# Three-product fp32r features for the last three heads of the mixer, split by ScalarE and GpSimd into the weight ring

## The reference, cut to what matters

```python
mod = cond @ w_ada[l] + b_ada[l]            # 6 x 1024 columns; the second block has 2 x 6144 more
h = modulate(x, norm1_w[l], shift1, scale1)
proj = h @ w_in                             # 256 x 1024 by 1024 x 3592
aq, ak, av, dqkv, dz, db, da = jnp.split(proj, IN_SPLITS, axis=-1)
attn_out = dilated_attention(aq, ak, av)    # 8 heads of 64
dqkv = silu(causal_short_conv(dqkv, conv_w))
o = gated_delta_rule(dq, dk, dv, g, beta)   # 4 heads of 128, chunks of 64
o = rms_norm(o, dn_norm_w) * silu(dz)
x = x + gate1 * (concat([attn_out, dn_out]) @ w_out)
```

## Time and profile before

| | us |
|---|---|
| median of 3 runs | 2387.39 (2383.18 to 2388.57) |
| profiled execution | 2388.36 |
| its span | 2386.6 |
| TensorE busy, whole span | 2180.7 |
| VectorE, ScalarE, GpSimd busy | 1373.6, 642.1, 123.7 |
| bytes moved | 711.73 MB, mean 298 GB/s |

### The profile page before, as it was taken

How to read it: one execution, slowest core, us unless ns; L and a number is a source line. 1 busy time by engine, 2 the same in 40 slices (tenths; PEclk the granted TensorE clock), 3 DMA queues, 4 the chain that set the end, 5 groups by cost and what they waited for, 6 DMA issues and landing times.

```text
span 2386.6 us, 40025 instructions
## 1 busy us (share of the span) xinstructions
PE 2180.7 (91%) x16396; PEld 1515.0 (63%) x16396; DVE 1373.6 (58%) x2654; ACT 642.1 (27%) x814; POOL 123.7 (5%) x203
## 2 busy tenths in 40 slices
PE   7998989998898998988999889899989999998998
PEld 5887842454545444445544555677769888876987
DVE  2455554634453443565545456866678676678866
ACT  1121120121222221311111111444443334445332
POOL 0000010000000000000000000000000000011000
PEclk9999989999999999999999999999989999999999
DMA  9778779998999999999999999444446533334651
GB/s 381 296 292 338 308 290 375 414 420 361 419 419 419 417 419 419 416 418 419 407 419 419 404 413 392 164 154 139 154 142 210 188 129 118 105 115 159 212 183 64
DMA packets 111244, 711.73 MB, mean 298 GB/s; under 512 B 12481, under 2 KB 13137, under 8 KB 36129
## 3 DMA queue, kind: packets, MB, share of 16 engines
q1 hardware_dynamic: 85904, 616.93, 65.4%
q0 software_dynamic: 25168, 92.38, 10.3%
HBM read 705.06 MB, written 4.19 MB: 297 GB/s over the span
## 4 chain that ended last, share of the span: by engine, by line
PE 67%; DVE 15%; DMA 13%; ACT 3%; issue 2%; SPq 0%; DVEq 0%; ACTq 0%
PE bank L313 17%; PE bank L2286 7%; PE bank L2267 6%; PE bank L1999 4%; PE bank L2037 4%; DMA hT<-in_panels_e 3%; PE bank L1662 3%; DMA cst<-in_panels_e 3%; PE bank L1512 2%; DMA ring<-in_units_a 2%; PE bank L2372 2%; DMA hid<-in_panels_e 2%; PE bank L2152 2%; PE bank L2014 2%; PE bank L2141 1%
## 5 line engine op out<-in xcount | busy, mean ns | idle before, releaser
L313 PE MATMUL bank<-hT,scratch 128*32 128x512 f32 x976 | 303.4, 609 | 11.9 <-DMA hT<-in_panels_e 10.0
L313 PE MATMUL bank<-hid,scratch 128*32 128x512 f32 x1008 | 308.0, 606 | 6.2 <-DMA hT<-in_panels_e 3.7
L1265 ACT CAST chi<-craw 128x1024 fp32r<-128x1024 f32 x128 | 133.6, 1045 | 550.9 <-DMA craw<-in_panels_m 214.2
L3290 DVE TENSOR_TENSOR clo<-craw,chi 128x1024 fp32r<-128x1024 f32 x128 | 156.0, 1222 | 158.8 <-ACT chi L1265 157.8
L313 PE MATMUL bank<-yacc,scratch 128*32 128x512 f32 x648 | 179.1, 609 | 5.0 <-DMA diag_gtmp<-in_panels_e 5.0
L313 PE MATMUL bank<-rows,scratch 128*32 128x512 f32 x632 | 172.9, 606 | 9.4 <-DMA cst<-in_panels_e 9.4
L313 PE MATMUL bank<-diag_gtmp,scratch 128*32 128x512 f32 x648 | 177.2, 600 | 2.2 <-DMA hid<-in_panels_e 1.5
L313 PE MATMUL bank<-cst,scratch 128*32 128x512 f32 x632 | 176.6, 608 | 2.4 <-DMA yacc<-in_panels_e 2.4
L1999 PE MATMUL bank<-cT_hi,chi 128*128 128x256 f32 x384 | 112.2, 292 | 17.4 <-DVE crot_lo L3264 6.1
L313 PEld LDWEIGHTS bank<-hT,scratch 128*32 128x32 f32 x976 | 70.7, 112 | 64.4 <-issue 63.8
L1999 PE MATMUL bank<-cT_lo,chi 128*128 128x256 f32 x384 | 109.2, 284 | 0.0
(11 more groups left out here) (680 smaller groups left out, 5680.3 us busy)
## 6 DMA issues: line engine op xcount, KB each, us to landing
hid<-in_panels_e SPq DMA_DIRECT2D x96, 1024.0 KB, 13.4
hT<-in_panels_e SPq DMA_DIRECT2D x94, 1024.0 KB, 13.5
ring<-in_units_a SPq DMA_DIRECT2D x88, 1024.0 KB, 7.1
ring<-in_panels_m SPq DMA_DIRECT2D x64, 1024.0 KB, 5.1
yacc<-in_panels_e SPq DMA_DIRECT2D x48, 1024.0 KB, 11.8
diag_gtmp<-in_panels_e SPq DMA_DIRECT2D x48, 1024.0 KB, 14.3
rows<-in_panels_e SPq DMA_DIRECT2D x47, 1024.0 KB, 13.2
cst<-in_panels_e SPq DMA_DIRECT2D x47, 1024.0 KB, 13.0
```

The costliest lines, as they stand in the source:

```text
L313: m = self.pe.matmul(b[s:s + STRIP, :], lhs(k)[:, s:s + STRIP], v, start=(first and k == 0), stop=(k == KT - 1))
L1265: act.copy(chi[:, h % 2, :], context_raw(h)).then_inc(cx_hi, 1)
L3290: tt(context_lower(h), context_raw(h), chi[:, h % 2, :], ALU.subtract).then_inc(cx_lo, 1)
```

## The change

For heads 1 to 3 the four halves of `first` and `second`, and for all four heads the feature half of `last_columns`, are computed with three fp32r products in place of one fp32 product: 16 halves, listed in `FEATURE_HALVES` in the order in which TensorE uses them. Head 0's first and second, all `tokens` products and all ada products stay in fp32. The tokens are split once: ScalarE copies `hT` into `x_hi`, GpSimd subtracts into `x_lo`, in two parts each. Each half of a weight is split when its unit has landed: ScalarE copies it into one of three places `first_hi`, GpSimd subtracts raw minus upper into `ring_lo[n % 4]`, and TensorE waits for GpSimd (`lower_in`) in place of the landing. ScalarE waits before the copy for the landing and for the use of the half three before it. The copies stand at fixed places of ScalarE's order: last of head 0 and first of head 1 ahead of the loop over j; second of head j + 1 between the Silus and Sqrt of j; last of j + 1 and first of j + 2 behind the Exp of the scores of j. `last_columns` does its tokens before its features. The later counts of `lower_in` and `upper_ready` are moved up by 18, and GpSimd's clearing of `b1raw` waits for the last changed unit, as `first_hi` lies in the same place.

```diff
@@ -73,6 +73,17 @@
+def feature_unit(kind, i):
+    return 8 + 12 * i + {"first": 0, "second": 6, "last": 9}[kind]
...
+FEATURE_HALVES = [(feature_unit(kind, i), half) for i in range(DN_HEADS)
+                  for kind, halves in (("first", 2), ("second", 2), ("last", 1)) if i or kind == "last" for half in range(halves)]
+ROW_PARTS = 2
+FRONT_PARTS = ROW_PARTS + len(FEATURE_HALVES)
...
 def first_units():
@@ -444,6 +455,8 @@
         ring_lo = sb("ring_lo", 4, UNIT, dt=F32R)
+        with ExitStack() as raw:
+            first_hi = raw.enter_context(nc.sbuf_tensor("first_hi", [P, 3, KT, P], F32R))
         with ExitStack() as raw:
@@ -462,6 +475,8 @@
         gateb = sb("gateb", 2, D)
+        with ExitStack() as stages:
+            x_lo = stages.enter_context(nc.sbuf_tensor("x_lo", [P, KT, SEQ], F32R))
         lnrow = sb("lnrow", 2, D)
@@ -569,6 +584,15 @@
         units = ring.rearrange("p s k (h n) -> p (s k h n)", h=2).rearrange("p (u k n) -> p u k n", u=4, k=KT)
+        x_hi = hT_lo[:, :, SEQ:512]
+        def first_parts(n, half):
+            lower = ring_lo[:, n % 4, :].rearrange("p (k n) -> p k n", k=KT)[:, :, P * half:P * half + P]
+            return first_hi[:, FEATURE_HALVES.index((n, half)) % 3], lower
+        def first_raw(n, half):
+            return units[:, n % 4, :, P * half:P * half + P]
@@ -1036,18 +1060,28 @@
+            for h in range(ROW_PARTS):
+                s = slice(4 * h, 4 * h + 4)
+                pool.wait_ge(upper_ready, h + 1)
+                pool.tensor_tensor(x_lo[:, s, :], hT[:, s, 0:SEQ], x_hi[:, s, :], ALU.subtract).then_inc(lower_in, 1)
+            for q, (n, half) in enumerate(FEATURE_HALVES):
+                upper, lower = first_parts(n, half)
+                pool.wait_ge(upper_ready, ROW_PARTS + q + 1)
+                pool.tensor_tensor(lower, first_raw(n, half), upper, ALU.subtract).then_inc(lower_in, 1)
             pool.wait_ge(b2_go, 1)
...
+            pool.wait_ge(unit_used, FEATURE_HALVES[-1][0] + 1)
             pool.memset(b1raw[64:P, :], 0.0).then_inc(filled, 1)
...
             for t in range(XT):
-                pool.wait_ge(upper_ready, t + 1)
+                pool.wait_ge(upper_ready, FRONT_PARTS + t + 1)
                 pool.tensor_tensor(xr_lo[:, t, :], xn[:, t, :], xr_hi[:, t, :], ALU.subtract).then_inc(lower_in, 1)
-            pool.wait_ge(lower_in, XT)
+            pool.wait_ge(lower_in, FRONT_PARTS + XT)
             pool.wait_ge(b1_upper, 1)
@@ -1161,6 +1195,21 @@
+            def upper_features(number):
+                for q in number:
+                    n, half = FEATURE_HALVES[q]
+                    act.wait_ge(first_in[n % 4], 16 * (n // 4 + 1))
+                    if q >= 3:
+                        act.wait_ge(unit_used, FEATURE_HALVES[q - 3][0] + 1)
+                    act.copy(first_parts(n, half)[0], first_raw(n, half)).then_inc(upper_ready, 1)
+            def halves_of(kind, i):
+                return [q for q, (n, _) in enumerate(FEATURE_HALVES) if n == feature_unit(kind, i)]
+            act.wait_ge(odd_feat.free, 2 + KT // 2)
+            act.wait_ge(side.free, 3 + KT // 2)
+            for h in range(ROW_PARTS):
+                act.copy(x_hi[:, 4 * h:4 * h + 4, :], hT[:, 4 * h:4 * h + 4, 0:SEQ]).then_inc(upper_ready, 1)
             act.wait_ge(small_in, 96)
@@ -1171,11 +1220,15 @@
             to_dve.send(act.activation(gates[:, 6, :], gates[:, 6, :], ACT.Exp))
+            upper_features(halves_of("last", 0) + halves_of("first", 1))
             for j in range(DN_HEADS):
+                more = j + 1 < DN_HEADS
                 asked.get()
                 to_tensor.send(act.activation(cs[:, :, :], cy[:, :, :], ACT.Silu))
+                if more:
+                    upper_features(halves_of("second", j + 1))
                 asked.get()
@@ -1187,6 +1240,10 @@
                 to_tensor.send(m)
+                if more:
+                    upper_features(halves_of("last", j + 1))
+                if j + 2 < DN_HEADS:
+                    upper_features(halves_of("first", j + 2))
@@ -1670,11 +1727,25 @@
+            def split_features(b, dst, n, half):
+                pe.wait_ge(lower_in, ROW_PARTS + FEATURE_HALVES.index((n, half)) + 1)
+                upper, lower = first_parts(n, half)
+                for k in range(KT):
+                    for c, (w, x) in enumerate(((upper, x_hi), (upper, x_lo), (lower, x_hi))):
+                        m = pe.matmul(b[:, dst:dst + SEQ], w[:, k, :], x[:, k, :], start=(k == c == 0), stop=(k == KT - 1 and c == 2))
+                return m
             def feature_pair(ready=lambda k: None):
...
                 G.close(features(b, SEQ, v, P), True)
+            def split_pair():
+                b = G.open()
+                n = G.panels.n
+                split_features(b, 0, n, 0)
+                G.close(split_features(b, SEQ, n, 1), True)
@@ -1685,9 +1756,9 @@
                 b = G.open()
-                v = first_unit(KT)
-                features(b, 0, v, 0)
-                G.close(tokens(b, SEQ, v, P), True)
+                n = G.panels.n
+                tokens(b, SEQ, first_unit(KT), P)
+                G.close(split_features(b, 0, n, 0), True)
@@ -1752,8 +1823,10 @@
                 later = 4 * i + 4
-                if more:
-                    feature_pair(*([] if i else [first_feature]))
+                if more and i:
+                    split_pair()
+                elif more:
+                    feature_pair(first_feature)
                 if i >= 2:
@@ -2089,7 +2164,7 @@
             from_experts.get()
-            pe.wait_ge(lower_in, XT)
+            pe.wait_ge(lower_in, FRONT_PARTS + XT)
             gather()
             turn_gathered(0)
```

## The result

| | changed | kernel before, runs beside it |
|---|---|---|
| median, us | 2397.57 (2393.75 to 2407.27, 8 runs) | 2387.65 (2383.18 to 2392.40, 8 runs) |
| profiled execution, us | 2400.66 | 2388.36 |
| its span, us | 2398.9 | 2386.6 |

The ratio is 1.0044, with a 95% interval from 1.0031 to 1.0057: slower, by 9.9 us of the medians. The forecast had +6.5 us (2393.9) and a range to 2402. All of it arises ahead of 207 us: `last_columns` of head 3, the last changed group, ends at 206.76 in place of 193.70, 13.1 us later, and 0.8 us of that are caught up by the end.

The account below looks back on a forecast made before the run. TensorE is busy, but the ring's loop (pair ends, three units land, next pair) is nearly as long. +4.2 us for the loop, +0.5 GpSimd, +1.8 clock make +6.5: 2393.9 us, range 2384 to 2402 for 8 in 10 runs.

Parts of the forecast that it names:

- What bounds the stage: Heads 0 to 3: TensorE busy, but pair end, three units landing, next pair nearly as long; slack 0.1 to 3.6 us.
- What TensorE saves: Changed halves: 2.87 us each, saving 0.78; a pair from 7.04 to 5.74 us; 10.9 us less work in all.
- The split: Cast and subtraction behind each landing: first product 3.7 us after it; second half's subtraction and those of last_columns hidden.
- The loop: End of head 0's second pair to end of the last pair: 124.3 us after, 119.3 before, +5.0 us.
- The casts in ScalarE's queue: Casts of "second" ahead of Sqrt and Exp: hidden by about a microsecond, 0 us; bound 1 us in each of three heads.
- GpSimd beside VectorE: Subtractions meeting VectorE's convolution at "first" pairs: GpSimd held up delays TensorE by 0.5 us, range 0 to 4.3.
- The clock: TensorE idling before the six pairs lowers its clock: one fall, 1.8 us; bounds 0 and three falls, 5.2 us.
- (2): Rival: landing delays shrink when transfers are asked for later, each loop up to 1.1 us shorter; -3 to +4 us; chance 0.24.
- (3): Rival: GpSimd waits out the convolution in "first" pairs of heads 1 and 3, clock falls twice more; +16 us; chance 0.14.
- (4): Rival: the split is ready when TensorE arrives, so its 10.9 us come through; faster, 2377 us; chance 0.07.
- (5): Rival: fp32r products run at a slower pitch, a tenth slower giving 3.2 us a half, +3.4 us more; chance 0.05.
- landing distances: End of a pair to landing of the next pair's unit, over six pairs: 67.6 us in all, taken as unchanged.

Follow-up runs that it names:

- the waits filled: Changed kernel plus unread fp32 products (3 to 8) ahead of TensorE's wait in each of the six changed pairs; 2392.22 us, 1.0016 of the kernel before.
- the split beside fp32 products: Changed kernel with casts and subtractions kept but unused, TensorE computing every half in fp32 from the raw unit; 2388.96 us, 0.9997 of the kernel before.
- the halves in two parts: Changed kernel with each half cast and subtracted in two parts of four k, TensorE waiting for each part; 2386.11 us, 0.9982 of the kernel before.
- the units six microseconds ahead: Changed kernel with ring places dealt out anew, the next pair's unit asked for first of three, not third; 2384.13 us, 0.9972 of the kernel before.
- places asked again early: Changed kernel with a changed pair's ring place asked for again once its unit is split, not used; 2395.95 us, 1.0030 of the kernel before.

## Why the prediction was right, and where it was short

- **What bounds the stage: right.** The ring's loop was nearly as long as TensorE's path, and anything put behind a landing lengthens it. All six pairs are now entered through transfer, cast and subtraction.
- **What TensorE saves: right.** A pair was forecast at 5.74 us and takes 5.89 at full clock. For a single half 2.84 us stand in the chain, where 2.87 were forecast.
- **The split: right.** Forecast 3.7 us from landing to first product, measured 3.63 to 3.71. The second half's subtraction was hidden under the first half, and `last_columns` was not held up. The lines of the cast and of the subtraction in the changed kernel:

```profile
L1204 ACT CAST first_hi<-ring x16: 1030/1041/1047, 66.9 to 196.5; 128x1024 fp32r<-128x1024 f32 x16
L1070 POOL TENSOR_TENSOR ring_lo<-ring,first_hi x16: 2339/2368/2439, 68.0 to 197.6; 128x1024 fp32r<-128x1024 f32 x16
```

- **The loop: right but for the clock.** 124.3 forecast (its three terms sum to 124.2); 124.7 with the waits filled.
- **The casts in ScalarE's queue: right, with a margin as thin as stated.** Nothing in the changed kernel; 1.9 us of waits for `arow` once TensorE came sooner, with the split beside fp32 products (1.2 and 0.75), and 0.7 with the halves in two parts. The bound given was up to 1 us in each head, so one of these is above it.
- **GpSimd beside VectorE: the term of 0.5 us was too much, at the wrong engine.** No subtraction took more than 2.44 us, where one alone takes 2.36. VectorE paid instead, with ten instructions of 2.1 to 2.5 us. The two groups of the convolution (ns), and one tensor_scalar in order of time, with the two subtractions beside it, of which the second starts at 102.65:

```profile
L2817 DVE TENSOR_SCALAR yacc<-gtmp,convcol x12: 341/350/2480, 77.7 to 212.0; 128x256 f32<-128x256 f32 x12
```

```profile
L2821 DVE SCALAR_TENSOR_TENSOR yacc<-gtmp,convcol,yacc x36: 473/480/2480, 80.6 to 215.8; 128x256 f32<-128x256 f32 x36
```

```profile
100.34 4.67 POOL L1070 TENSOR_TENSOR ring_lo<-ring,first_hi 128x1024 fp32r<-128x1024 f32 x2 [17.50 <-ACT first_hi L1204]
...
102.98 2.12 DVE L2857 TENSOR_SCALAR hid<-yacc,xn 128x128 f32<-128x128 f32 x1
```

  An instruction of 0.35 or 0.48 us takes as long as a whole subtraction. In all ten cases the subtraction had begun first, 0.1 to 0.5 us before, and VectorE's instruction ended when it ended, to within 0.3 us. The prediction had this hidden, and it is: TensorE's waits for GpSimd in the stretch 66 to 198 us are 16.2 us, for VectorE 2.0, as before the change. The Trainium skill (SBUF — State Buffer, section "Who interferes with whom") has the pair of ports as a lock that one of the two holds for a whole instruction; these rows agree.
- **The clock: the step that was mis-sized.** "I take one, 1.8", with three falls as the upper bound. There were four, 5.8 us in the pairs, and with the waits filled the pairs are 5.3 us shorter. The price of one was near: 1.45 us for 1.7. The fall in the kernel before was twice as long, with half of it ahead of the pair, and the 3.4 us that met the pair, from 55.69, are what each of the four brought. Its granted clock:

```profile
52.25:59.07 6.82, 6.27 (x44) 5.10 (x45) 0.70 (x4) 2.69 (x4) 0.00 (x0) 0.50 0.98 404
```

  The idle times that the step had worked out (3.3, 4.2, 0.9, 2.0, 2.1, 3.5) came out as 3.23, 4.03, 1.76, 2.54, 1.61, 3.03; the mistake was to take one fall out of a range although three of the idle times were twice the 1.70 us of the earlier trace rows, and to end the range at three when two more (2.0 and 2.1) were above 1.70 as well. One of those two met a fall.
- **The rivals.** (2), landing tails that vanish, did not happen: first to third landing of a triple still takes 6.3 to 7.2 us (before, 6.2 on average; the prediction has 6.1). (3), GpSimd losing against VectorE, did not, for the reason above. (4), the split hidden, is false of this ring and true of another: with the units six microseconds ahead, the kernel is faster than before by 4 us, less than half of the 10.9 us of work that was to come through. (5), a slow pitch: 5.89 for 5.74 is 2.6% and 0.9 us over the six pairs, not a tenth.

The misses, summed at the end of the last changed half, where the profiled execution is 13.1 us late and 6.5 were forecast: pairs at the lower clock 5.8, longer pairs 0.9, landing distances 1.2 (67.0 to 70.2 over the six kernels with the old order of places and no early asking, and the longest has no fall of the clock), split -0.3, `last_columns` of head 3 0.2, and 1.1 of head 0's second pair, which the change doesn't touch (7.1 to 10.2 us over the profiles of all these kernels). That is 8.9, less the 2.3 us that the forecast had set aside for clock and GpSimd: 6.6. The medians, with 9.9 us, are nearer to the forecast than the one profiled execution. That they come within 3.4 us of it is in part luck: the 0.5 us set aside for GpSimd wasn't needed and stood in for some of the clock.

What stays open: why the clock falls at one idle time and not at another (below), and why the landing distances differ by up to 3 us between these six kernels.

## What to carry to other kernels

Before an operand is given a preparation step (a cast, a split), read how long its data lie ready before they are used; here it was 0.1 to 3.6 us at pairs of 7 us, and a preparation of 3.7 us cost more than the 1.3 us a pair that the quicker products save. If the data come through a ring, the order in which places are dealt out decides that slack: the unit with a preparation must be asked for first, and then the same edit is a gain. And a new wait of TensorE should be priced with the clock that it may cost, once for each long wait (here four of six met a fall) and not once for the stage.

## What the runs showed of the hardware

- Falls of the granted clock from 2.4 to 1.2 GHz, each 3.4 us long, cost a pair of fp32r halves some 1.45 us. In the changed kernel they followed idle times of 2.54 to 4.03 us and not those of 1.61 and 1.76. The idle time just before isn't all of it: where places are asked again early, a pair behind 3.00 us ran at full clock and one behind 2.51 did not, and with the halves in two parts one behind 1.89 us did not. The first two pairs of the kernel with places asked again early, in the timeline:

```profile
80.04 0.36 PE L1744 MATMUL bank<-hT_lo,first_hi 128*128 128x256 f32 x1 [3.00 <-POOL first_lo L1078]
...
99.21 0.55 PE L1744 MATMUL bank<-hT_lo,first_hi 128*128 128x256 f32 x1 [2.51 <-POOL first_lo L1078]
```

- Filling an idle TensorE with three to eight fp32 products ahead of each pair (0.44 us each at full clock) kept the clock up through the whole stage. It is a probe, and only half a remedy: three of the pairs then started behind the filling.
- Where GpSimd and VectorE met, VectorE paid here: ten instructions took 2.1 to 2.5 us, while no subtraction grew by more than 0.1 us. In the earlier trace rows each had lost once.
